# A squared-ReLU MLP by seven products for eight, in three token blocks for five

## The reference

```python
    h = x + jnp.concatenate([attn_out, lru_out], axis=-1) @ w_out
    hn = rmsnorm(h, norm_ffn_g)
    y = h + jnp.square(jax.nn.relu(hn @ w_up)) @ w_down    # w_up 1024 x 4096, w_down 4096 x 1024
```

## Time and profile before

| quantity | value |
|---|---|
| median of three runs | 2170.88 us (2170.09 to 2173.76) |
| span of the profiled execution | 2169.7 us |
| TensorE busy | 2107.5 us, 97% |
| TensorE weight loads busy | 2005.8 us, 92% |
| VectorE busy | 1144.0 us, 53% |
| ScalarE busy | 912.9 us, 42% |
| GpSimd busy | 214.1 us, 10% |
| data moved by DMA | 270.91 MB, mean 125 GB/s |

### The profile page before, as it was taken

One profiled execution on the slowest core, in us unless ns is written; L12 is line 12 of the kernel. 1 busy time (PEld: TensorE's weight loads), 2 busy tenths in 40 slices (PEclk: granted clock), 3 DMA queues, 4 the chain that ended last, 5 costly groups with the idle time before them and its releaser, 6 DMA issues.

```text
span 2169.7 us, 29768 instructions
## 1 busy us (share of the span) xinstructions
PE 2107.5 (97%) x11299; PEld 2005.8 (92%) x11299; DVE 1144.0 (53%) x1547; ACT 912.9 (42%) x1530; POOL 214.1 (10%) x163
## 2 busy tenths in 40 slices
PE   7899999999999999999999999999999999999998
PEld 6788787887887999999999999999999999999997
DVE  6777668666687644335543346443364433444323
ACT  5655646556465443224432234422244322444222
POOL 2121302212112300003000002000030000000000
PEclk9999999999999999999999999999999999999999
DMA  5442342332434433334533344433354333353332
GB/s 155 114 146 84 108 131 85 121 114 75 131 110 152 154 117 117 118 117 159 164 117 117 117 153 134 151 109 117 118 166 157 118 117 117 124 162 119 122 117 73
DMA packets 253547, 270.91 MB, mean 125 GB/s; under 512 B 10483, under 2 KB 241427, under 8 KB 253427
## 3 DMA queue, kind: packets, MB, share of 16 engines
q1 hardware_dynamic: 253427, 269.24, 39.1%
HBM read 251.99 MB, written 17.32 MB: 124 GB/s over the span
## 4 chain that ended last, share of the span: by engine, by line
PE 82%; issue 8%; DVE 4%; ACT 2%; POOL 2%; DMA 1%; SPq 0%; POOLq 0%; DVEq 0%; ACTq 0%
PE results L1185 46%; PE scores_a L1185 17%; PE bank L1185 17%; PE aux L1310 1%; DVE w_lo L857 1%; POOL prob L538 1%; PE aux L1381 1%; ACT w_hi L581 1%; DVE xg_lo L875 1%; DMA raw<-in_w_up 0%; POOL ix L533 0%; DVE xc L1033 0%; DMA raw<-in_w_in 0%; ACT prob L646 0%; POOL sumsq L514 0%
## 5 line engine op out<-in xcount | busy, mean ns | idle before, releaser
L862 DVE TENSOR_TENSOR w_lo<-raw,w_hi 128x1024 fp32r<-128x1024 f32 x320 | 397.5, 1242 | 794.7 <-ACT w_hi L587 794.7
L587 ACT ACTIVATE w_hi<-raw 128x1024 fp32r<-128x1024 f32 x320 | 337.9, 1056 | 469.0 <-PE scores_a L1185 244.9
L1185 PE MATMUL results<-hn_hi,w_hi 128*128 128x416 f32 x1280 | 448.0, 350 | 1.8 <-DVE w_lo L862 0.8
L1185 PE MATMUL results<-hn_hi,w_lo 128*128 128x416 f32 x1280 | 449.2, 351 | 0.0
L1185 PE MATMUL results<-hn_lo,w_hi 128*128 128x416 f32 x1280 | 447.4, 350 | 0.0
L821 ACT ACTIVATE act_t<-results 128x416 f32<-128x416 f32 x160 | 82.7, 517 | 396.4 <-PE results L1185 396.3
L1185 PEld LDWEIGHTS results<-hn_hi,w_hi 128*128 128x128 f32 x1280 | 240.3, 188 | 3.7 <-DVE w_lo L862 1.2
L1185 PEld LDWEIGHTS results<-hn_lo,w_hi 128*128 128x128 f32 x1280 | 240.3, 188 | 2.5
L1185 PEld LDWEIGHTS results<-hn_hi,w_lo 128*128 128x128 f32 x1280 | 240.3, 188 | 0.2
L1185 PE MATMUL scores_a<-hid_hi,w_hi 128*128 128x416 f32 x640 | 224.7, 351 | 2.6 <-issue 2.6
L1185 PE MATMUL scores_a<-hid_hi,w_lo 128*128 128x416 f32 x640 | 224.6, 351 | 0.0
(11 more groups left out here) (192 smaller groups left out, 2936.3 us busy)
## 6 DMA issues: line engine op xcount, KB each, us to landing
raw<-in_w_up SPq DMA_DIRECT2D x160, 512.0 KB, 4.7
raw<-in_w_down SPq DMA_DIRECT2D x160, 512.0 KB, 4.4
raw<-in_w_in SPq DMA_DIRECT2D x70, 512.0 KB, 4.9
raw<-in_w_out SPq DMA_DIRECT2D x30, 512.0 KB, 4.5
hnext<-h_scratch SPq DMA_DIRECT2D x5, 1664.0 KB, 10.0
hcur<-h_scratch SPq DMA_DIRECT2D x5, 1664.0 KB, 10.0
h_scratch<-hacc SPq DMA_DIRECT2D x8, 896.0 KB, 5.6
out<-yout SPq DMA_DIRECT2D x17, 416.0 KB
```

What stands on the lines that cost most here:

```text
L587: nc.scalar.activation(like_unit2(w_hi[n % 2]), raw_unit2(n % U2), ACT.Copy).then_inc(w_hi_done, 1)
L862: nc.vector.tensor_tensor(like_unit2(w_lo[n % 2]), raw_unit2(n % U2), like_unit2(w_hi[n % 2].bitcast(F32)), ALU.subtract).then_inc(w_lo_do ...
L1185: last = nc.tensor.matmul(out, wt, x(kx), start=(start and i == 0 and part == 0), stop=(stop and i == len(ks) - 1 and part == 2))
```

## The change

The MLP now takes three blocks of 696 tokens (starting at tokens 0, 692 and 1384, so that four tokens are done twice at each seam). Both products of a block are split into two halves along rows, columns and tokens, and one level of the Strassen-Winograd scheme is applied: of the 8 quarter products, 7 are left, on sums and differences of the quarters. A block is 32 units (`Unit`), in groups of four: two `up` units and two `down` units (`u.r` is 0 to 3). A unit is 7 products `k` of 12 matmuls of 348 columns. Each unit needs 7 weight forms of 512 columns, of which ScalarE makes `w2_hi` (`weights_high`) and VectorE `w2_lo` (`weights_low`) in four instructions (`u.ops`). Four of the 7 forms are sums: in block 0 GpSimd makes them (`sums_of`), they are stored to the DRAM tensor `s_scratch` (`store_s`), and blocks 1 and 2 load them. `w2_lo` lies on the same memory as the raw weights and sums, so in block 0 VectorE waits for the store before it overwrites them.

In `up` three of the products' running sums are copied out of PSUM by ScalarE (x1, x5, x2) and added to by VectorE; they become the four quarters b11, b22, b12, b21 of the hidden tile. GpSimd makes four differences of these (`hidden_forms`), and all 7 forms are split again. In `down` VectorE adds 7 running sums, two tiles at a time, into `hcur` (`add`). The norm of the next block is made piece by piece in the background. The whole MLP is written out without loops.

```diff
-B2 = 416
-NB2 = TOKENS // B2
...
+NH = 348
+TB = 2 * NH
+NB2 = 3
+STEP = 692
+UN = 32
...
+        self.q = self.r % 2
+        lead = g % 2
+        self.ops = [(0, 1), (1, 3), (3, 5), (5, 7)] if lead else [(0, 2), (2, 4), (4, 6), (6, 7)]
...
+                u = Unit(g)
+                if part in (1, 3) and not u.first:
+                    half = part // 2
+                    sp.wait_ge(s_out[u.s][half], 16 * (u.i // 2 + 1))
+                    sp.dma_start(raw_slots(u, 1 + 3 * half, 2), s_dram[u.i][:, 2 * half:2 * half + 2, :])\
+                      .then_inc(w2_in[u.s][part], 16)
...
+                    dst = w2_raw[u.s][:, k, :].rearrange("p (c n) -> p c n", c=4 if u.up else 2)
+                    sp.dma_start(dst, quarter(u, k)).then_inc(w2_in[u.s][part], 16)
+            def store_s(g, half):
+                u = Unit(g)
+                sp.wait_ge(s_done, 4 * g + 2 * half + 2)
+                sp.dma_start(s_dram[u.i][:, 2 * half:2 * half + 2, :], raw_slots(u, 1 + 3 * half, 2))\
+                  .then_inc(s_out[u.s][half], 16)
...
+            def after(g, k):
+                u, nxt = Unit(g), Unit(g + 2)
+                sp.wait_ge(prod_done, u.product(k))
...
+                if k in parts and nxt.g < G:
+                    load_part(nxt.g, parts[k])
+                if Unit(g + 1).first and k in (2, 4):
+                    store_s(g + 1, (k - 2) // 2)
+                if u.b and u.i < 2:
...
+            def sums_of(g):
+                u = Unit(g)
+                w, count = w2_raw[u.s], 16 * (g // 2 + 1)
+                pool.wait_ge(w2_in[u.s][3], count)
+                pool.wait_ge(w2_in[u.s][4], count)
+                nc.gpsimd.tensor_tensor(w[:, 1, :], w[:, 4, :], w[:, 6, :], ALU.add).then_inc(s_done, 1)
+                pool.wait_ge(w2_in[u.s][0], count)
+                pool.wait_ge(s_done, 4 * g + 1)
+                nc.gpsimd.tensor_tensor(w[:, 2, :], w[:, 1, :], w[:, 0, :], ALU.subtract).then_inc(s_done, 1)
+                nc.gpsimd.tensor_tensor(w[:, 4, :], w[:, 0, :], w[:, 4, :], ALU.subtract).then_inc(s_done, 1)
+                pool.wait_ge(w2_in[u.s][2], count)
+                pool.wait_ge(s_done, 4 * g + 2)
+                nc.gpsimd.tensor_tensor(w[:, 5, :], w[:, 3, :], w[:, 2, :], ALU.subtract).then_inc(s_done, 1)
...
+            def hidden_forms(g):
...
+                pool.wait_ge(b12_done, n + 1)
+                pool.wait_ge(sq_done, 3 * n + 1)
+                nc.gpsimd.tensor_tensor(hid_form(q, 1), b12[:, :], b11, ALU.subtract).then_inc(t_done, 1)
+                pool.wait_ge(sq_done, 3 * n + 2)
+                pool.wait_ge(t_done, 4 * n + 1)
+                nc.gpsimd.tensor_tensor(hid_form(q, 2), b22[:, :], hid_form(q, 1), ALU.subtract).then_inc(t_done, 1)
+                pool.wait_ge(sq_done, 3 * n + 3)
+                pool.wait_ge(t_done, 4 * n + 2)
+                nc.gpsimd.tensor_tensor(hid_form(q, 6), b21[:, :], hid_form(q, 2), ALU.subtract).then_inc(t_done, 1)
+                nc.gpsimd.tensor_tensor(hid_form(q, 4), b22[:, :], b12[:, :], ALU.subtract).then_inc(t_done, 1)
...
+            for g in range(G):
+                u = Unit(g)
+                if u.r in (1, 2):
+                    hidden_forms(g - 1)
...
+                if g + 1 < UN:
+                    sums_of(g + 1)
...
+            def weights_high(g, j):
...
+                if 7 * g + hi - 1 >= 8:
+                    act.wait_ge(prod_done, 7 * g + hi - 1 - 8 + 1)
+                for k in range(lo, hi):
+                    if k in (0, 3, 6):
+                        act.wait_ge(w2_in[u.s][{0: 0, 3: 2, 6: 4}[k]], 16 * (g // 2 + 1))
...
+                at = u.slot(lo)
+                nc.scalar.activation(w2_hi[:, at:at + hi - lo, :], raw_slots(u, lo, hi - lo), ACT.Copy).then_inc(whi_done, 1)
...
+            def last_quarter(g):
+                u = Unit(g)
+                act.wait_ge(prod_done, u.product(6))
+                square_relu(u.n, 2, bank(u, 6), b21[:, :])
...
+                hidden_high(u.n, 1)
+            def up(g):
+                u = Unit(g)
+                n, prev = u.n, u.r == 1
+                if prev:
+                    last_quarter(g - 1)
...
+                act.wait_ge(prod_done, u.product(0))
...
+                nc.scalar.activation(x1, bank(u, 0), ACT.Copy).then_inc(held_done, 1)
...
+                if prev:
+                    hidden_high(n - 1, 2)
+                    hidden_high(n - 1, 3)
+                act.wait_ge(prod_done, u.product(1))
+                nc.scalar.activation(x5, bank(u, 1), ACT.Copy).then_inc(held_done, 1)
...
+                if prev:
+                    hidden_high(n - 1, 6)
+                    hidden_high(n - 1, 4)
+                act.wait_ge(prod_done, u.product(2))
+                act.wait_ge(b12_done, n)
+                nc.scalar.activation(x2, bank(u, 2), ACT.Copy).then_inc(held_done, 1)
...
+                weights_high(g + 1, 0)
+                act.wait_ge(added, 3 * n + 1)
+                square_relu(n, 0, x1, b11)
+                hidden_high(n, 0)
...
+                weights_high(g + 1, 1)
+                act.wait_ge(added, 3 * n + 2)
+                square_relu(n, 1, x5, b22[:, :])
+                hidden_high(n, 5)
...
+                weights_high(g + 1, 2)
+                weights_high(g + 1, 3)
+            def down(g):
+                u = Unit(g)
+                n, prev = u.n + 1, u.r == 2
+                if prev:
+                    last_quarter(g - 1)
+                weights_high(g + 1, 0)
+                if prev:
+                    hidden_high(n, 2)
+                    hidden_high(n, 3)
...
+                weights_high(g + 1, 1)
+                if prev:
+                    hidden_high(n, 6)
+                    hidden_high(n, 4)
...
+            def weights_low(g, j):
...
+                dve.wait_ge(whi_done, 4 * g + j + 1)
+                if u.first:
+                    if lo < 4:
+                        dve.wait_ge(s_done, 4 * g + (3 if hi <= 2 else 4))
+                    for half in range(2):
+                        if any(lo <= k < hi for k in (1 + 3 * half, 2 + 3 * half)):
+                            dve.wait_ge(s_out[u.s][half], 16 * (u.i // 2 + 1))
+                at = u.slot(lo)
+                nc.vector.tensor_tensor(w2_lo[u.s][:, lo:hi, :], raw_slots(u, lo, hi - lo),
+                                        w2_hi.bitcast(F32)[:, at:at + hi - lo, :], ALU.subtract).then_inc(wlo_done, 1)
...
-                    split2(b, j + 2)
-                    dve.wait_ge(sq_done, 32 * b + j + 1)
-                    nc.vector.tensor_copy(hid_hi[:, j, :], act_t[:, j % 2, :]).then_inc(hid_hi_done, 1)
-                    dve.wait_ge(hid_hi_done, 32 * b + j + 1)
-                    nc.vector.tensor_tensor(hid_lo[:, j, :], act_t[:, j % 2, :], hid_hi.bitcast(F32)[:, j, :], ALU.subtract)\
-                      .then_inc(hid_lo_done, 1)
...
+            def up(g):
...
+                if prev:
+                    for k in (1, 2, 3, 6, 4):
+                        hidden_low(n - 1, k)
...
+                if not Unit(g + 1).first:
+                    weights_low(g + 1, 0)
+                dve.wait_ge(held_done, 3 * n + 1)
+                dve.wait_ge(prod_done, u.product(3))
+                nc.vector.tensor_tensor(x1, bank(u, 3), x1, ALU.add).then_inc(added, 1)
...
+                hidden_low(n, 0)
+                dve.wait_ge(held_done, 3 * n + 2)
+                dve.wait_ge(prod_done, u.product(4))
+                nc.vector.tensor_tensor(x5, bank(u, 4), x5, ALU.add).then_inc(added, 1)
...
+                hidden_low(n, 5)
+                weights_low(g + 1, 0 if Unit(g + 1).first else 1)
+                dve.wait_ge(held_done, 3 * n + 3)
+                dve.wait_ge(prod_done, u.product(5))
+                nc.vector.tensor_tensor(x2, bank(u, 5), x2, ALU.add).then_inc(added, 1)
+                dve.wait_ge(added, 3 * n + 3)
+                dve.wait_ge(t_done, 4 * n)
+                nc.vector.scalar_tensor_tensor(b12[:, :], x2, 0.0, x2, ALU.max, ALU.mult).then_inc(b12_done, 1)
...
+                if Unit(g + 1).first:
+                    weights_low(g + 1, 1)
+                weights_low(g + 1, 2)
+                weights_low(g + 1, 3)
+            def down(g):
...
+                if prev:
+                    hidden_low(n, 1)
+                else:
+                    add(g - 1, 6)
+                add(g, 0)
+                if prev:
+                    hidden_low(n, 2)
+                    hidden_low(n, 3)
+                add(g, 1)
+                if prev:
+                    hidden_low(n, 6)
+                    hidden_low(n, 4)
+                elif not first:
+                    weights_low(g + 1, 0)
+                add(g, 2)
+                add(g, 3)
+                if prev and not first:
+                    weights_low(g + 1, 0)
...
+                add(g, 4)
+                weights_low(g + 1, 0 if first else 1)
+                add(g, 5)
```

(43 more changed lines are left out.)

885 lines of the change are left out of this document (574 added, 311 removed).

## The result

The changed kernel takes **2404.4 us** (median of 4 runs, 2399.6 to 2407.2), the kernel before 2171.9 us: a ratio of 1.107, 95% interval 1.105 to 1.109. The prediction was 2258 us within 2100 to 2330: the sign was right, the size was not, and the time lies outside the range. The profiled execution has a span of 2405.4 us, 235.7 more than before and 147.8 more than the sum said.

The account below looks back on a forecast made before the run. It took TensorE's number of matmuls and their distance as the bound. From 2169.7 us: -160.1 matmuls, -3 transposes, +10 start, +8 seams, +3 tail, +13 norm, +207 waits, +10 clock = 2257.6, called 2258 us, range 2100 to 2330.

Parts of the forecast that it names:

- matmuls of 348 columns: TensorE's MLP products: 8064 matmuls 159.0 ns apart, 1282.2 us for 1442.3, taking off 160.1 us.
- the walk: One four-unit group followed step by step: TensorE waits 6.9 us in blocks 1 and 2, 15.0 in block 0; 207 in all.
- the clock: TensorE at half clock after waits of 3.4 us or more, once in each of 24 groups: 10 us, between 0 and 38.
- background norm: Next block's norm in VectorE's stream, about half falling into units where VectorE is late: 13 us for two blocks.
- start: Seven input forms of 1392 columns made at the start, so TensorE is fed late: 10 us, between 2 and 20.
- seams: Same input-form work laid over unit 31 at the two seams: 4 us each, 0 to 10.
- end: The tail after the products: six tiles for four, three of them started early: 3 us.
- rival 5: Matmul distances follow the skill page's rule, all else as in the likeliest case: 93 us less, 2165 us; chance 0.02.
- rival 2: Only block 0 stalls, since GpSimd's differences in later blocks find VectorE's gaps: 2149 us, 2100 to 2166; chance 0.20.
- rival 3: Nearly all waits hidden, 1.2 us per group left without any lock: 2070 us, up to 2100; chance 0.12.
- the likeliest case: Waits in the groups are 0.55 to 1.3 of the walk's: 2178 to 2330 us; chance 0.53.
- Rival 4: SyncE's single queue and 512-byte pieces of `w_up` make weights late in block 0 too: about 2400 us; chance 0.08.

Follow-up runs that it names:

- run 15: Changed kernel with the next block's norm left out in blocks 0 and 1 (its loads for unit 30 stay): 2370.5 us (1.092).
- run 1: Changed kernel with each of the 12 seam stores of output rows carrying 16 rows of 116: 2370.8 us (1.092).
- run 6: Changed kernel with four tiles instead of two for finished output rows at a seam, full stores: 2377.3 us (1.094).
- run 7: Changed kernel with 20 idle matmuls of 164 columns before the second half of product 1 in each group's third unit: 2398.0 us (1.105).
- run 9: Changed kernel with each store of 116 output rows cut in two, 112 and 4 rows (those of 112 into 96 and 16): 2359.2 us (1.085).
- run 2: Changed kernel with GpSimd's four differences of the hidden tiles 8 columns wide instead of 348, the forms split from b12: 2295.7 us (1.056).
- run 3: Changed kernel with no sums of weights made or stored; block 0 loads quarters like blocks 1 and 2: 2343.1 us (1.079).
- run 10: Changed kernel with GpSimd's work on the input forms in four instructions of 348 columns each instead of one of 1392: 2386.4 us (1.099).
- run 11: Changed kernel with the edits of run 5, run 6, run 9 and run 10, plus further reordering of VectorE's low parts, differences and additions: 2220.4 us (1.023).
- run 12: Run 11 with GpSimd's 128 sums of weights in block 0 in two instructions of 256 columns each: 2206.4 us (1.015).
- run 13: Run 12 with two input differences at the start moved to VectorE, ScalarE's first copy earlier, VectorE reordered at seams and in third units: 2184.2 us (1.006).
- run 16: Run 13 with the next block's norm moved inside the units, behind ScalarE's splits and VectorE's low parts, same arithmetic: 2161.8 us (0.996).
- run 14: Run 13 with no sums of weights made or stored: 2121.1 us (0.977).
- run 5: Changed kernel with the hidden tiles' differences on VectorE and the order of VectorE's and ScalarE's work changed: 2317.8 us (1.068).
- run 17: Run 16 with GpSimd's input work in halves of 696 columns instead of quarters of 348: 2173.0 us (1.000).

## Why the prediction was wrong

Step by step, measured on the changed kernel unless a run is named.

| step | predicted, us | measured, us |
|---|---|---|
| matmuls of 348 columns, 159.0 ns each | -160.1 | 12 in 1.90 to 1.92: 159 ns, right |
| the walk and the clock in regular groups | 207 + 10 | 16 x 7.7 + 8 x 14.9 = 242: about 179 of waits, 63 of the clock |
| background norm | 13 | 34 (run 15) |
| start | 10 | 18 before the first matmul, 12 in the first group |
| seams | 8 | 2 x 38 in first groups, 12 in the units ahead of them (17.6 and 22.4 us for 14.7 and 13.3): 88 |
| end | 3 | 21 |

The misses, 25 + 21 + 20 + 80 + 18, make 164 for the 148 that are missing: the terms overlap, and the start is uncertain by some us (the first matmul came at 704.2 to 709.4 us in runs 1, 6, 7 and 9, whose start is the same).

In short, the steps that failed are the seams (8 us for 88), the clock (10 for 75, over all groups), and the start, the norm and the end (26 for 85).

**The distance** was right, by the line through the earlier trace rows; so rival 5 is out. The Trainium skill ("TensorE: Matmul & The Clock Gate", "Back-to-back issue gap") would have 147.5 ns here by the rule that the prediction uses. The section gives that rule for an isolated matmul, and for a stream of matmuls with their own weight loads 131 ns at 512 columns, which the prediction left out. The trace disagrees with both: 159 ns at 348 columns.

**The walk** was right in place, and near in size by luck. It said 6.9 us of waits a group in blocks 1 and 2 and 15.0 in block 0. Measured are 5.7 and, where no norm disturbs them (run 15), 11.0: eight tenths and seven tenths of the walk, where I took nine. The clock behind these waits took another 2.0 and 3.9 us a group, where the sum had 0.4. The two errors nearly cancel: the groups lost 7.7 (61.1 - 53.4) and 14.9 us, 242 in all for 217. Runs 2 and 3 take away one side of the contention each, and the groups fall by 5.1 and by about 7 us; rivals 2 and 3 are out, since every group of blocks 1 and 2 stalls too. A slip of the prediction beside this: 1.3 times the walk's 230 us would put the upper end of the likeliest case at 2350 us, not 2330; 2404 is beyond either.

**Seams: the largest step that failed.** The prediction had "At the two seams the same work lies over unit 31: +4 each, 0 to 10". I costed the seven input forms and did not cost the old block's output: six tiles through two places, each with a store. The list no store of output rows, and I did not ask when one lands. It is 9.5 to 9.8 us, three on the path (the third of 112 rows, slow beside the loads of weights). Runs 1, 6 and 9 each attack that wait in another way (smaller stores, more places, faster stores), and each brings a first group from 99 to 81 to 86 us: TensorE's two waits for a place fall from 5.3 and 8.1 us to 2.9 and 1.5 in all three, the one for `hid_y` from 11.3 to 4.6, 7.9 and 7.8. Part of the rest is VectorE and GpSimd on 1392 columns at once, which run 10 shortens (99 to 94 or 95 us); with the order in runs 11 to 13 it comes to 69 to 74. What each change of order gave was not taken apart.

**The end** was sized as three tiles' work; it is six tiles' stores, five of them with 116 rows on about a quarter of the DMA engines. Run 9 takes 19 us off it.

**The start** I bounded by 20 and it was 30. GpSimd's forms, 3.2 us alone by my own line, took up to 8.3 beside VectorE; I had the contention in the walk and left it out of this term. Run 13 bears it out: 10 us from two differences made by VectorE, with a copy of ScalarE's moved forward.

**The norm** was priced by VectorE's work alone, half of it hidden. ScalarE's squares stand at the start of a unit, ahead of the relu that TensorE waits for, and SyncE's queue waits for them too. Run 16 moves them and 22 us return. How much of the 34 each part has was not measured.

**The clock.** The loss by distances of 200 to 330 ns is 75.5 us over the MLP (618 of 8063 distances, each less 159 ns), not 10, and beyond the 38 that I gave as the upper end. I had counted one wait of 3.4 us a group, up to 1.6 us lost behind it, and taken a quarter of that. A regular group of block 2 already lost 2.0 us, the second to seventh of block 0 lost 3.4 to 5.0 each, where several waits follow each other, and the three first groups 4.9 to 6.4. Behind the seam's wait of 11.3 us:

```profile
1367.00:1368.00 1.00, 0.00 (x0) 0.00 (x0) 0.36 (x1) 0.89 (x2) 0.00 (x0) 0.50 0.03 8
1368.00:1369.00 1.00, 0.79 (x3) 0.79 (x4) 1.00 (x3) 0.89 (x3) 0.00 (x0) 0.50 0.00 0
...
1372.00:1373.00 1.00, 1.00 (x5) 1.00 (x4) 0.78 (x2) 0.18 (x1) 0.00 (x0) 0.50 0.00 0
1373.00:1374.00 1.00, 1.00 (x7) 1.00 (x7) 0.36 (x1) 0.00 (x0) 0.00 (x0) 0.88 0.00 0
```

five us at half clock (1.2 GHz), then back. It is a price of the waits rather than a cause: run 7 fills some and gains 6 us, and in run 16, with 126 us of waits for 304, it is 22.5.

**Rival 4** gave 2400, the time that came, by another mechanism: late weights. TensorE waits 1.4 us for weights in six groups of block 0, and 139 of the missing us lie outside regular groups, so that mechanism did not make the time. Through the sums it may have a share in block 0 (run 3). A time that fits is no evidence.

**Left open:** why a group of block 0 still takes 9 us more than one of block 2 in run 16. The sums are the cause (run 14), but whether through VectorE's waits for GpSimd, ScalarE's waits for the sums or the waits for stores was not taken apart.

## What to carry to other kernels

Walk not only the loop's steady group but its first and last: here 139 of those 164 us lay where one block hands over to the next, at both ends, and in work that runs beside. For every buffer that is written again, ask when its last store lands, and read that time off a store of the same number of rows. Where an in-order engine is late, first see whether ready and urgent work stands behind work that waits or is not yet needed: order alone was worth 78 us in run 5 and 22 in run 16, and with the rest it made of a loss of 10.7% a gain of 0.4%.

## What the runs showed of the hardware

**Rows of a store.** A store of 116 rows of 4 KB ran at 87 to 101 GB/s with the DMA engines 25% busy; as 112 and 4 rows at 242 to 289 GB/s, 67 to 88% busy. That looks like 4 of 16 engines, and 4 is the largest number up to 16 that divides 116. The kernel before stores 104 rows: from 2163 to 2165 us, with nothing else moving, at 274 and 311 GB/s and 81 to 85% busy, and 13 of 16 would be 81%. Only these were compared, so this is a pattern in three cases and not a rule shown.

**What waits for GpSimd.** In run 16, VectorE beside GpSimd's sums (one row for 8 of them):

```profile
1130.51 0.85 DVE L1579 TENSOR_TENSOR hid_lo<-hid_raw,hid_hi 128x348 fp32r<-128x348 f32 x1
1131.28 1.04 DVE L1594 TENSOR_TENSOR hid_raw<-b,hid_raw 128x348 f32<-128x348 f32 x1
1132.25 0.87 DVE L1607 TENSOR_TENSOR hcur<-aux,hcur 128x696 f32<-128x696 f32 x1
...
1138.76 0.87 DVE L1607 TENSOR_TENSOR hcur<-aux,hcur 128x696 f32<-128x696 f32 x1
1139.55 0.51 DVE L1579 TENSOR_TENSOR hid_lo<-hid_raw,hid_hi 128x348 fp32r<-128x348 f32 x1
```

```profile
1128.61 7.92 POOL L789 TENSOR_TENSOR w_raw<-w_raw 128x256 f32<-128x256 f32 x8 [5.45 <-DMA w_raw<-in_w_down]
```

While the sums run, until 1136.5, instructions of 348 columns with two operands in SBUF take 0.85 to 1.05 us, and 0.51 afterwards; the addition out of PSUM takes 0.87 in both. The Trainium skill ("SBUF — State Buffer", "SBUF: two separate sides") says that the lock is taken by VectorE with two SBUF inputs, against a GpSimd instruction that reads SBUF; the trace agrees. It follows that the length of GpSimd's instructions matters and not only their sum: halves of the sums took 14 us off (run 12 against 11), quarters of the input work 18 (run 10) and 11 against halves (run 16 against 17).
